# adaLN weight quarters of a two-layer encoder moved from the FFN loops into the waits of the norms, with buffers of their own for the first loads and the first units' splits

## What is computed

```python
mod = jax.nn.silu(c) @ w_ada + b_ada                       # (9 sequences) x (9 * 1024) per layer
sh1, sc1, ga1, sh2, sc2, ga2, sh3, sc3, ga3 = split(mod, 9)
h = rms_norm(x, gains[0]) * (1 + sc1) + sh1
x = x + 0.5 * ga1 * rms_norm(swiglu(h, w_f1_in, w_f1_out), gains[1])
h = rms_norm(x, gains[2]) * (1 + sc2) + sh2
y = token_mixing(h, ..., w_in, ..., w_out)                 # three kinds of attention
x = x + ga2 * rms_norm(y, gains[3])
h = rms_norm(x, gains[4]) * (1 + sc3) + sh3
x = x + 0.5 * ga3 * rms_norm(swiglu(h, w_f2_in, w_f2_out), gains[5])
```

## Time and profile before

| | |
|---|---|
| three runs | 1807.21, 1809.58, 1818.76 us, median 1809.58 |
| the profiled execution | 1810.48 us, of which the span from first to last instruction is 1808.9 us |
| mean granted TensorE clock | 0.941 |
| PE busy | 1650.7 us, 91% of the span |
| DVE, ACT, POOL busy | 838.4, 580.3, 171.1 us |
| DMA moved | 265.87 MB, mean 147 GB/s |

### The profile page before, as it was taken

The page is one execution under the profiler, slowest core; times in us unless marked ns, Lnnn a source line. Parts: engine busy times, 40 slices in busy tenths (PEclk is TensorE's granted clock), DMA queues, the critical chain, the costliest instruction groups (busy, mean ns, idle before and its releaser), DMA issues.

```text
span 1808.9 us, 26074 instructions
## 1 busy us (share of the span) xinstructions
PE 1650.7 (91%) x10150; PEld 1483.8 (82%) x10150; DVE 838.4 (46%) x1187; ACT 580.3 (32%) x753; POOL 171.1 (9%) x233
## 2 busy tenths in 40 slices
PE   4899999979958799999979999997998697999998
PEld 2799988779947699998869999886987576999986
DVE  1534433363775744343364434326455666444424
ACT  2333322334244422222243323224244324222222
POOL 4000010010033100000010000101001421000000
PEclk7899999989967899999989999998998688999999
DMA  7776783332303267543337777642432243444332
GB/s 263 221 228 195 224 264 131 116 105 84 127 24 115 76 210 212 160 117 138 117 118 224 217 242 227 204 140 70 126 96 70 65 126 95 138 134 121 127 129 82
DMA packets 252685, 265.87 MB, mean 147 GB/s; under 512 B 11679, under 2 KB 216605, under 8 KB 252610
## 3 DMA queue, kind: packets, MB, share of 16 engines
q1 hardware_dynamic: 230512, 183.52, 33.5%
q0 software_dynamic: 22080, 81.26, 13.3%
q10 hardware_dynamic: 18, 0.04, 0.0%
HBM read 258.70 MB, written 6.09 MB: 146 GB/s over the span
## 4 chain that ended last, share of the span: by engine, by line
PE 81%; DVE 9%; ACT 5%; DVEq 2%; DMA 1%; issue 1%; ACTq 0%
PE ps L1527 18%; PE ps L1529 17%; PE ps L1528 17%; PE ps L1566 6%; PE ps L1568 6%; PE ps L1570 6%; PE ps L1496 4%; DVE x L1112 2%; DMA w_ada_sb<-in_w_ada_dram 1%; ACT w_hi L777 1%; DVE w_lo L1070 1%; DVE qa_bd L1207 1%; PE ps L1727 1%; ACT square_out L801 1%; PE ps L1857 1%
## 5 line engine op out<-in xcount | busy, mean ns | idle before, releaser
L1527 PE MATMUL ps<-act_hi,w_hi 128*128 128x384 f32 x1792 | 611.8, 341 | 27.2 <-DVE act_lo L1097 22.7
L1529 PE MATMUL ps<-act_hi,w_lo 128*128 128x384 f32 x1792 | 603.4, 337 | 0.0
L1528 PE MATMUL ps<-act_lo,w_hi 128*128 128x384 f32 x1792 | 603.0, 336 | 0.0
L1070 DVE TENSOR_TENSOR w_lo<-w_raw,w_hi 128x2048 fp32r<-128x2048 f32 x158 | 362.1, 2292 | 241.6 <-ACT w_hi L784 201.4
L1527 PEld LDWEIGHTS ps<-act_hi,w_hi 128*128 128x128 f32 x1792 | 340.0, 190 | 52.4 <-issue 43.0
L1528 PEld LDWEIGHTS ps<-act_lo,w_hi 128*128 128x128 f32 x1792 | 340.2, 190 | 0.0
L1529 PEld LDWEIGHTS ps<-act_hi,w_lo 128*128 128x128 f32 x1792 | 339.5, 189 | 0.0
L784 ACT ACTIVATE w_hi<-w_raw 128x2048 fp32r<-128x2048 f32 x126 | 241.2, 1914 | 227.5 <-PE ps L1570 227.4
L1149 DVE TENSOR_TENSOR hid_f<-silu_g,ps 128x384 f32<-128x384 f32 x88 | 48.8, 554 | 415.0 <-ACT silu_g L841 415.0
L841 ACT ACTIVATE silu_g<-ps 128x384 f32<-128x384 f32 x88 | 43.3, 492 | 529.3 <-PE ps L1529 529.2
L1566 PE MATMUL ps<-w_hi,hid_hi 128*128 128x512 f32 x528 | 163.9, 391 | 0.0
(11 more groups left out here) (359 smaller groups left out, 1338.3 us busy)
## 6 DMA issues: line engine op xcount, KB each, us to landing
w_raw<-in_w_ffn_in_dram SPq DMA_DIRECT2D x176, 512.0 KB, 5.1
w_ada_sb<-in_w_ada_dram POOLq DMA_DIRECT2D x64, 1024.0 KB, 5.5
w_raw<-in_w_ffn_out_dram SPq DMA_DIRECT2D x88, 512.0 KB, 4.2
w_raw<-in_w_in_dram SPq DMA_DIRECT2D x46, 512.0 KB, 4.6
w_ada_sb<-in_w_ada_dram SPq DMA_DIRECT2D x8, 1024.0 KB, 7.3
w_raw<-in_w_out_dram SPq DMA_DIRECT2D x16, 512.0 KB, 4.6
k_sb_raw<-in_cache_k_sb_dram POOLq DMA_DIRECT2D x2, 1024.0 KB, 6.6
va_past<-in_cache_v_sb_dram POOLq DMA_DIRECT2D x2, 1024.0 KB, 6.4
```

The costliest lines, as they stand in the source:

```text
L1070: dve.tensor_tensor(w_lo[slot][:], w_raw[slot][:], w_hi[slot][:].bitcast(F32), ALU.subtract).then_inc(lo_ready.sem, 1)
L1527: pe.matmul(out, w, a, start=first, stop=False)
L1528: pe.matmul(out, w, al, start=False, stop=False)
L1529: return pe.matmul(out, wl, a, start=False, stop=last)
```

## The change

Eighteen components are counted through, in the order of their work. 0 and 1 are the head (now scale first, then shift). Four run in layer 0's first FFN loop, two in layer 1's, two in layer 0's second FFN. The other eight run in the five norms: two in the norm behind a first FFN (both layers), one in the norm behind the attention (both layers), two in the norm behind layer 0's second FFN. `R0`, `R1` are the old two buffers; `S0` and `G0` to `G4` lie over memory that is not in use at that time.

```diff
+    PT_BANK = (0, 1, 2, 3)
+    IN_BANK = (4, 2)
+    ADA_BANK, ADA_BANK_B = 6, 7
+    HEAD = 2
+    LOOP_F1 = ((0, 2, 4), (1, 4, 2))
+    GAP_F1 = ((6, 7), (6, 7))
+    GAP_OUT = 8
+    LOOP_F2 = (0, 1)
+    GAP_F2 = (2, 3)
+    R0, R1, S0, G0, G1, G2, G3, G4 = range(8)
+    TWO = (R0, R1, R0, R1)
+    ADA_SLOT = [(R0, R1, S0, G0), (G1, G2, G3, G4)]
+    ADA_SLOT += [TWO] * 4 + [(R0, R1, S0, G1), (G2, G0, G3, R0)]
+    ADA_SLOT += [(R0, R1, G0, G1)]
...
+        first_hi = put("first_hi", [P, 2048], F32R)
+        first_lo = put("first_lo", [P, 2048], F32R)
```

SP issues the eight head quarters with no wait between them (layer 0's first unit between the fourth and the fifth). POOL's loads:

```diff
+                def ada_gap(n, layer, components, u0):
+                    m = 4 * n
+                    ada_load(m + 2, layer, components[0])
+                    ada_load(m, layer, components[0])
+                    ada_load(m + 1, layer, components[0])
+                    for k, units in ((3, 3), (4, 6), (5, 8), (6, 8)):
+                        pool.wait_ge(unit_used.sem, unit_used.at(l, u0 + units))
+                        ada_load(m + k, layer, components[k // 4])
+                    ada_load(m + 7, layer, components[1])
...
-                pool.wait_ge(ada_used.sem, ada_used.at(l, 4 * ADA_F2))
+                pool.wait_ge(ada_used, 4 * N_GAP2[l])
                 pass_gate()
                 pool.dma_start(k_sb_raw[:],
...
-                first_split(l, U_WIN)
...
                 pool.wait_ge(kt_tr.sem, kt_tr.at(l, 8))
-                ada_component(ADA_F2, l, 8, (0, 1))
-                first_split(l, U_F2IN)
-                ada_component(ADA_F2, l, 8, (2, 3))
+                ada_load(4 * N_GAP2[l], l, GAP_OUT)
+                ada_load(4 * N_GAP2[l] + 1, l, GAP_OUT)
+                pool.wait_ge(gla_gated.sem, gla_gated.at(l, HB))
+                pool.wait_ge(gla_mm.sem, gla_mm.at(l, HB))
+                pool.wait_ge(rows_stored.sem, rows_stored.at(l, 10))
+                pool.wait_ge(states_stored.sem, states_stored.at(l, 4))
+                ada_load(4 * N_GAP2[l] + 2, l, GAP_OUT)
+                ada_load(4 * N_GAP2[l] + 3, l, GAP_OUT)
```

`m + 7` goes to a buffer that `m` (or `m + 1`) used, so it waits for that quarter's matmuls. ACT writes `act_hi` itself, from PSUM, and splits the first unit ahead of the norm:

```diff
                         scale, shift = mod[:, 3 * nth + 1, f, 0:1], mod[:, 3 * nth, f, 0:1]
+                        act.activation(act_hi[:, f, 0:NP], prompt_chunk(f), ACT.Identity, scale=scale, bias=shift)
                         act.activation(y[:, f, :], prompt_chunk(f), ACT.Identity, scale=scale, bias=shift).then_inc(y_ready.sem, 1)
...
                     sum_new_x(nth, 0)
-                    if nth == 0:
-                        act.wait_ge(gate_cols_landed.sem, gate_cols_landed.at(l, 1))
-                    split_hi(u, u % 2)
                     sum_y(nth, 1)
...
                 proj_out(U_F1OUT, KF // 2, ahead=False)
-                renorm(0, U_WIN)
+                act.wait_ge(gate_cols_landed.sem, gate_cols_landed.at(l, 1))
+                split_first_hi(U_WIN, U_F1OUT + 6)
+                renorm(0)
```

DVE takes the first units' `w_lo` from POOL, ahead of its `renorm`, and no longer casts `act_hi`:

```diff
                 proj_out(U_F1OUT, KF // 2, 0)
+                split_first_lo(U_WIN)
                 renorm(0)
...
                     for f in range(KD):
                         dve.wait_ge(y_ready.sem, y_ready.at(l, nth * KD + f + 1))
-                        dve.tensor_copy(act_hi[:, f, 0:NP], y[:, f, :])
-                        dve.drain()
                         dve.tensor_tensor(act_lo[:, f, 0:NP], y[:, f, :], act_hi[:, f, 0:NP].bitcast(F32),
                                           ALU.subtract).then_inc(act_ready.sem, 1)
```

In the head DVE scales the samples and subtracts the first unit's `w_lo` while the second component is still being loaded. The `params_t` copies, the bias additions and the gain folds of what the norms computed follow the first unit behind the norm (`read_params`, `add_gap1` to `add_gap3`). PE:

```diff
+                def four_hidden(u0, h0, norm, j, quarters, mods_before, after_first, first=False):
+                    hidden(u0, h0, norm, j, 0, first)
+                    after_first()
                     hidden(u0, h0, norm, j, 1)
-                    ada_quarter(l, nth, 1)
-                    ada_quarter(l, nth, 2)
+                    pe.wait_ge(mod_ready, mods_before)
+                    quarters(range(0, 2))
                     hidden(u0, h0, norm, j, 2)
-                    ada_quarter(l, nth, 3)
                     hidden(u0, h0, norm, j, 3)
-                    ada_transpose(l, nth)
+                    quarters(range(2, 4))
...
                     products(1, 2).then_inc(unit_used.sem, 1)
+                    n = (N_GAP1[l], N_GAP2[l], N_GAP3)[nth]
+                    pe.wait_ge(gate_read.sem, gate_read.at(l, 2 * nth + 2))
+                    ada_quarters(n, range(4))
                     pe.wait_ge(x_normed.sem, x_normed.at(l, TT * nth + 2))
                     transpose_prompts(0, range(KD))
                     pe.wait_ge(x_normed.sem, x_normed.at(l, TT * nth + 3))
                     for g in range(4):
                         transpose_prompts(1, (2 * g, 2 * g + 1)).then_inc(prompt_tr.sem, 1)
+                    if nth != 1:
+                        ada_quarters(n + 1, range(4), ADA_BANK_B)
```

More of the change, by code:

```diff
@@ L622, in _ @@
                     load_head(l + 1)
-                def ada_component(nth, layer, component, quarters=range(4)):
-                    for q in quarters:
-                        pool.wait_ge(ada_used.sem, ada_used.at(l, nth * 4 + (q - 1)))
-                        pass_gate()
-                        pool.dma_start(w_ada_sb[q % 2][:],
-                                       T["w_ada"][layer, q * 256:(q + 1) * 256, bass.ds(component * 1024, 1024)]
-                                       .rearrange("(k p) n -> p k n", p=P)).then_inc(ada_landed[q % 2].sem, 16)
@@ new lines, in ada_loop @@
+                def ada_loop(n0, layer, component, count):
+                    with pool.Fori(0, count) as i:
+                        for q in range(4):
+                            slot = ADA_SLOT[n0][q]
+                            pool.wait_ge(ada_used, i * 4 + (4 * n0 + q - 1))
+                            pass_gate()
+                            pool.dma_start(w_ada_slot[slot][:],
+                                           T["w_ada"][layer, q * 256:(q + 1) * 256, bass.ds(i * 1024 + component * 1024, 1024)]
+                                           .rearrange("(k p) n -> p k n", p=P)).then_inc(ada_landed[slot], 16)
@@ L740, in _ @@
             u_even.credit(act)
-            ada_rows_ready.credit(act)
             act.wait_ge(c_zeroed, 1)
@@ L1902, in _ @@
                 if l < LAST:
-                    pe.wait_ge(head_landed.sem, head_landed.at(l, 1))
-                    pe.matmul(ps[:, 1, 0:24], head, ident[0:24, 0:24], start=True, stop=True).then_inc(head_tr.sem, 1)
-                four_hidden(U_F2IN, KF, 2, 0, ADA_F2)
-                if l < LAST:
-                    with pe.Fori(0, 2) as i:
-                        four_hidden(U_F2IN, KF, 2, i * 4 + 4, i + (ADA_F2 + 1))
-                plain = KF - 12 if l < LAST else KF - 4
-                with pe.Fori(0, plain // 2) as i:
+                    for g in range(len(LOOP_F2)):
+                        four_hidden(U_F2IN, KF, 2, 4 * g, lambda qs: ada_quarters(N_F2 + g, qs), N_F2 + g,
+                                    after_first_f2 if g == 0 else lambda: ada_transpose(N_F2), first=(g == 0))
+                    done = 8
+                    hidden(U_F2IN, KF, 2, done, 0)
+                    ada_transpose(N_F2 + 1)
+                else:
+                    done = 0
+                    hidden(U_F2IN, KF, 2, done, 0, first=True)
+                    after_first_f2()
+                hidden(U_F2IN, KF, 2, done, 1)
+                with pe.Fori(0, (KF - done - 2) // 2) as i:
                     for s in range(2):
-                        hidden(U_F2IN, KF, 2, i * 2 + (KF - plain), s)
+                        hidden(U_F2IN, KF, 2, i * 2 + (done + 2), s)
                 proj_out(U_F2OUT, KF // 2, KF, 2)
```

433 lines of the change are left out of this document (274 added, 159 removed).

## The result

The changed kernel takes **1732.43 us** (median of 4 runs, 1730.18 to 1733.98) beside 1810.39 for the kernel before on the same chip (1807.21 to 1818.76): ratio 0.9565, interval 0.9545 to 0.9584. The forecast was 1737 in a range of 1727 to 1760. The profiled execution is the run of 1730.18, with a span of 1728.2.

The account below looks back on a forecast made before the run. PE's own work (81% of the chain) and its standing time bound the kernel; 16.6 head + 37.7 loops + 14.3 - 2.5 norms + 6.5 clock = 72.6 us less than 1810.48, forecast 1737 us, range 1727 to 1760.

Parts of the forecast that it names:

- Head: Start of kernel: last quarter arrives at 30.6, first unit at 38.1 for 55.35, 17.2 us less.
- Loops: FFN loops: components' quarters go from 70.7 us to 33.0, eight remaining, all in pairs: 37.7 us less.
- the head's put-off work: Params transpose and mask matmuls move from a wait to behind the first unit in PE's run: about 0.6 us back.
- Norms, the wait: Five norms: DVE's x update no longer slowed beside POOL's w_lo, first unit 2.7 us earlier each, plus 0.8: 14.3 us.
- Norms, what is put in: Five norms: quarters that run over, moved splits and late w_lo cost 0.5 us per norm: -2.5 us, bounds 0 and -10.
- just fit: Three norms: second four quarters, 370.5 to 374.5, end before the first unit at 374.6; 1 us over costs 3 in all.
- The 1.2 us that the prediction took from it: Norms: POOL's eighth-quarter load could be blocked by one DVE L1076, up to 1.2 us more, still landing at 373.2.
- Clock: First units behind norms: 4.5 us gained behind FFNs by no clock fall, half of 4.2 behind the attention: 6.5 us.
- 1: Norms: clock falls all the same because narrow quarters don't hold it; 6.2 us a norm in three, 1758 us; chance 0.15.
- 2: Norms: quarters' loads or splits come late, 3 us in each norm, 1752 us; chance 0.09.
- 3: Slower than before: cache load behind the norm lands late, PE's key transposes wait in each layer, 1827 us; chance 0.02.
- 4: Quarters in the norms cost what they cost in the loops, 33 us come back, 1770 us; chance 0.03.

Follow-up runs that it names:

- short quarters: Changed kernel with 24 of 32 quarters each cut to one 8-column matmul: in the norms 1738.63 us (0.9619), in the loops 1717.28 us (0.9474).
- the second batch behind the attention: Changed kernel with one component moved from layer 0's second FFN loop to the norm behind its attention: 1741.69 us; loads held until the unit's weights landed, 1732.18.

## Why the prediction was right

- **Head, forecast 17.2, measured 16.0.** The step that was off is the arrival of the last quarter, 30.6 in the forecast and 33.1 in the trace. 390 GB/s for everything was the wrong picture: the quarters moved at 411, the unit between them at 290, and 0.6 MB of later loads moved before the last quarter was complete. The path behind it was right (7.5 us from the quarter's start, 7.38 to 7.39 in the six profiles whose last quarter ran at half clock); the fast last quarter (1.07 for 1.94) was not forecast, gave 1.1 back, and is luck. The buffers carry the head, which is shown: 11.4 of the 16.0. The Trainium skill (DMA: Bandwidth & Descriptors, "Where 436 GB/s comes from") gave an arrival of 33.1 by its 358 GB/s. The time agrees by accident, the reason doesn't: the window shows 379, and 411 while only quarters moved.
- **Loops, forecast 37.7.** The four FFN stages gave 9.6, 5.0, 20.1 and 4.1 for the sums 9.9, 5.1, 18.2 and 4.5 of the prediction; the 0.6 of the head's put-off work and a fast first unit (20.1 for 18.2) would explain the two that differ most. The worth of a loop's quarter, 0.8 us, is measured by itself; the prediction's 1.03 in a pair was somewhat high.
- **Norms, the wait, forecast 14.3.** 2.86, 3.25, 3.32, 2.87 and 2.84 make 15.1. The mechanism, POOL's operation beside DVE's update, is shown by putting it back (3.98 us) and by running it earlier on the same engine (1.28).
- **Norms, what is put in, forecast -2.5.** Not spent: the norms are as long with short quarters as with whole ones, because a quarter takes 0.87 in a row, not 1.00, and the batches end 0.24 us ahead of what DVE needs. That the second batch would "just fit" was right to a quarter of a microsecond, at full clock. Beside a DVE that worked on, the late load landed in time (at 345.8 in the first norm, used from 347.56): the Trainium skill's rule on the shared port (SBUF — State Buffer, "Who interferes with whom") cost nothing here that a wait shows. The 1.2 us that the prediction took from it have the wrong operation behind them: L1076 has one of its inputs in PSUM, and by that section such an operation leaves the shared port free. Its other half, that the blocked side waits for the whole instruction, fits the update's 3.98, which ended 1.07 us behind POOL's 4.61, while the gating (L1206, one input from PSUM) kept its 0.68 beside it.
- **Clock, forecast 6.5.** Behind the FFN norms it is 1.00 over 344 to 360, 893 to 909 and 1191 to 1207, as said. Behind the attention it is 0.89 and 0.79 (593 to 609, 1439 to 1455): over the first 16 us of the first unit 0.89 and 0.84, where it was 0.87 and 0.86 before, so the 2.1 us booked there did not come. "PE never idle for more than 1 us in the three full norms" was wrong: PE stands 1.85 to 2.57 us ahead of the samples' transposes there, and in some executions the clock fell at that place. That filling a wait keeps the clock up is shown by the second batch behind the attention (0.89 to 1.00, some 1.6 to 1.8 us) and spoken for by the times of the short quarters; for the 4.5 us of the FFN norms the size stays unproved, since their part in the attention stages hides in the scatter.
- **Rivals.** 1 did not come about in the changed kernel (the norms' quarters ran at full clock), but its mechanism is real: it cost up to 1.7 us a norm in the kernel with POOL's split in the norm, and a dip of 1.4 us was seen in the changed kernel itself. 2 fell: PE waits for no quarter's load in a norm. A late load was made only by the kernel that queued four in front of a unit's weights, and there the weights came late and not the quarters. 3 fell: the cache's keys landed 6.6 us behind their issue at 349.54. 4 fell by the two kernels with short quarters.

The sum by stages, 72.7 against 80.7 in the profiled execution: -1.2 head, +3.3 norms (0.8 gained more, 2.5 not spent), +7.7 attention, and -1.9 in the FFN stages, mostly clock booked there and not seen. So nearly all of the surplus is the attention stages, whose gain can't be put down to the change, and the profiled runs, a slightly slow one before and the fastest after, stretch it: the medians give 78.0 and, for the changed kernel taken again, 74.8.

## What to carry to other kernels

Independent work of the busiest engine belongs into the waits that that engine has anyway, and it is free to within what a trace of PE's waits gives: fill each wait up to the time at which the other engine is ready, and no further (0.24 us left here; four quarters more cost 3.2). It can give more than its own time, since the work behind a filled wait found the clock full (0.89 to 1.00 behind the attention). Its loads must be issued early enough, but not queued in front of a load that stands on the path (ACT's wait for the weights grew by 8.7 us here): order them behind that load's landing. And a long two-input operation on GpSimd, like the 4.6 us split here, is to be moved to where VectorE has nothing long to do, whichever engine then runs it.

## What the hardware showed that I had not expected

- Loads issued later from the same engine moved before the earlier ones had landed: 0.6 MB of them in the head. What they cost isn't shown.
- Loads in 512 B packets moved at 290 GB/s (18 to 20 us), loads in 4 KB packets at 411 (8 to 16 us), both with the queue full.
- The same wait of PE (2.57 and 2.53 us, same norm, same code) left the clock full in one execution and at half in another, 1.4 us apart in the norm.
- The attention stage's clock differed by 0.05 and its length by 7 us between two kernels with the same matmuls there (0.92 and 0.87), more than most of these experiments were meant to show.
- Each of ACT's activations out of PSUM is recorded with 0.56 to 0.63 us, but the next starts 0.45 later, so two results per chunk cost 0.90; DVE's subtraction kept up.
- SP's 0.5 MB loads, issued 4 us after four 1 MB loads of POOL's queue, needed until 14 us after their first issue to land, for a median of 5.1 in the changed kernel.
